# Value products of six cached sequences as two-part fp32r products, split by GpSimd and spread over the pages

## The reference

```
for one sequence:                                 # 8 of them
    ckv = cache_ckv[pages]   (2048, 256) + new (8, 256)
    k   = rmsnorm([ckv @ w_uk | kpe])             # per head, 8 heads
    s   = q . k * SCALE, causal mask
    p   = softmax(s)                              # (8 heads x 8 queries, 2056)
    o_lat = p @ ckv                               # (64, 256): the value product
    o     = o_lat @ w_uv
```

## Time and profile before

| | |
|---|---|
| runs | 1563.53, 1565.51, 1567.21 us; median 1565.51 |
| span of the profiled execution | 1561.6 us, 3.9 us under the median |
| PE busy | 1546.7 us (99%) |
| DVE, ACT, POOL busy | 1042.6, 631.2, 581.8 us |
| granted TensorE clock, mean | 0.998 |
| cached sequences | about 717.5 to 1041.6 us of the span |
| time of the profiled execution itself | not given apart from its span; by the median it would be 1561.6 + 3.9 us |

### The profile page before, as it was taken

How to read it: one execution, slowest core, us unless ns; L and a number is a source line. 1 busy time by engine, 2 the same in 40 slices (tenths; PEclk the granted TensorE clock), 3 DMA queues, 4 the chain that set the end, 5 groups by cost and what they waited for, 6 DMA issues and landing times.

```text
span 1561.6 us, 31760 instructions
## 1 busy us (share of the span) xinstructions
PE 1546.7 (99%) x11182; PEld 1475.9 (95%) x11182; DVE 1042.6 (67%) x1672; ACT 631.2 (40%) x1192; POOL 581.8 (37%) x604
## 2 busy tenths in 40 slices
PE   8999999999999999999999999999999999999998
PEld 8999999999999999588988888888999999999998
DVE  4998888512269975866777777774759988885011
ACT  6444445422221242464654445552434444354110
POOL 3165555445445654320000000013551655554342
PEclk9999999999999999999999999999999999999999
DMA  6133334223223332002122222212222333342222
GB/s 173 51 101 92 94 94 124 69 80 87 80 77 103 83 112 73 1 1 72 52 62 62 61 62 62 58 45 81 82 81 58 105 94 94 94 118 67 75 82 72
DMA packets 231405, 122.29 MB, mean 78 GB/s; under 512 B 28399, under 2 KB 228311, under 8 KB 231300
## 3 DMA queue, kind: packets, MB, share of 16 engines
q1 hardware_dynamic: 230238, 120.30, 27.4%
q10 hardware_dynamic: 1070, 0.74, 0.2%
HBM read 117.79 MB, written 3.58 MB: 78 GB/s over the span
## 4 chain that ended last, share of the span: by engine, by line
PE 93%; DVE 3%; issue 1%; ACT 1%; DMA 1%; SPq 0%; DVEq 0%; ACTq 0%
PE ps L474 40%; PE ps L1439 27%; PE ps L1790 12%; PE ps L1724 4%; PE ps L1710 2%; PE ps L1581 1%; PE ps L1635 1%; PE ps L1610 1%; PE ps L1753 1%; DMA x_nat<-in_x_sample 1%; PE ps L1625 1%; PE ps L1587 1%; PE ps L1592 0%; DVE xs L1999 0%; DVE xs_raw L1984 0%
## 5 line engine op out<-in xcount | busy, mean ns | idle before, releaser
L460 POOL TENSOR_TENSOR w_lobuf<-w_rawbuf,w_hibuf 128x256 fp32r<-128x256 f32 (+2 forms) x336 | 316.8, 974 | 355.1 <-ACT w_hibuf L453 355.1
L1439 PE MATMUL ps<-xs,w 128*128 128x288 f32 x3192 | 427.5, 296 | 2.2 <-DVE w L1913 2.2
L1439 PEld LDWEIGHTS ps<-xs,w 128*128 128x128 f32 x3192 | 426.8, 188 | 2.6 <-issue 2.6
L756 POOL TENSOR_TENSOR w<-w_raw,w 128x256 fp32r<-128x256 f32 x216 | 222.6, 1062 | 222.9 <-DVE w_raw L1901 139.2
L453 ACT ACTIVATE w_hibuf<-w_rawbuf 128x1024 fp32r<-128x1024 f32 (+1 forms) x90 | 104.8, 1164 | 359.6 <-PE ps L474 358.2
L474 PE MATMUL ps<-a_hi,w_hibuf 128*128 128x288 f32 x704 | 152.6, 297 | 0.0
L474 PE MATMUL ps<-a_hi,w_lobuf 128*128 128x288 f32 x704 | 152.1, 297 | 0.0
L474 PE MATMUL ps<-a_lo,w_hibuf 128*128 128x288 f32 x704 | 150.2, 294 | 0.0
L474 PE MATMUL ps<-x_hi,w_hibuf 128*128 128x288 f32 (+1 forms) x672 | 146.1, 299 | 1.6 <-DVE w_lobuf L2073 0.8
L474 PE MATMUL ps<-x_hi,w_lobuf 128*128 128x288 f32 (+1 forms) x672 | 144.5, 296 | 0.0
L474 PE MATMUL ps<-x_lo,w_hibuf 128*128 128x288 f32 (+1 forms) x672 | 144.4, 296 | 0.0
(11 more groups left out here) (320 smaller groups left out, 2722.7 us busy)
## 6 DMA issues: line engine op xcount, KB each, us to landing
w_raw<-in_ffn_w_gu SPq DMA_DIRECT2D x76, 256.0 KB, 2.9
up_rows<-in_ffn_w_gu SPq DMA_DIRECT2D x74, 256.0 KB, 3.1
c_nat<-in_cache_ckv SPq DMA_DIRECT2D x128, 128.0 KB, 2.0
w_rawbuf<-in_w_in SPq DMA_DIRECT2D x58, 256.0 KB, 3.1
w_rawbuf<-in_ffn_w_down SPq DMA_DIRECT2D x32, 384.0 KB, 4.0
w_rawbuf<-in_ffn_w_down SPq DMA_DIRECT2D x32, 320.0 KB, 3.4
w_rawbuf<-in_ffn_w_gu SPq DMA_DIRECT2D x24, 256.0 KB, 3.3
w_rawbuf<-in_w_out SPq DMA_DIRECT2D x16, 256.0 KB, 3.1
```

Source lines behind the costliest of these rows:

```text
L460: ins = pool.tensor_tensor(w_lobuf[:, r, part], w_rawbuf[:, r, part], w_hibuf[:, r % HIS, part].bitcast(F32), ALU.subtract)
L756: ins = pool.tensor_tensor(w7[b][:, slot, 1, part], w7_raw[b][:, slot, 1, part], w7[b][:, slot, 0, part].bitcast(F32), ALU.subtract)
L1439: mm = pe.matmul(ps[:, seven_bank(f, slot), 0:HALF], m, xs[:, slot, n, k, :], start=k == 0 and j == 0, stop=k == KH - 1 and j == 2)
```

## The change

For sequences r = 0 to 5 (those whose softmax runs inside s = 1 to 6, `stacked`), the value product becomes fp32r. The exponentials are written twice: rounded to fp32r in `p_two[..., 0, :]` and in fp32 in `s_buf`; GpSimd subtracts and writes the low part to `p_two[..., 1, :]`. High and low together are one stationary operand of 128 columns. GpSimd also splits each page pair of `c_nat` into `c_hi` (four buffers) and `c_lo` (in place). Each page is then two fp32r matmuls (`c_hi`, `c_lo`) of 256 columns; rows 0 to 63 and 64 to 127 of the result are added at the end. The eight pairs are spread over pages 10 to 14. Sequences 6 and 7 keep the fp32 product. The loads of the first two merge pieces move behind the last page load, and their splits into the last sequence.

```diff
+        STACKED = NS - 2
+        PAIRS, EARLY_PAIRS = NP // 2, len(c_hi)
...
-            for t in range(2):
-                load_merge(t)
...
-                        sp.wait_ge(pages_used, used + (g + 1))
+                        sp.wait_ge(pages_used, used + 2 * (g + 1))
...
+            sp.wait_ge(lat_mm, STACKED)
+            for t in range(2):
+                load_merge(t)
...
+            pool.sem_inc(pages_used, EARLY_PAIRS)
...
+            def split_pair(r, b, j):
+                two = slice(2 * j, 2 * j + 2)
+                made = 2 * j + (1 if j < EARLY_PAIRS else 3)
+                pool.wait_ge(ct_tr, r * PAIRS + (j + 1))
+                pool.wait_ge(pages_used, r * PAIRS + (j + 1))
+                pool.tensor_tensor(c_hi[j % EARLY_PAIRS][:, :, :], c_nat[:, b, two, :], ones[:, 0:1, None].broadcast_to([P, 2, KL]), ALU.mult).then_inc(split_made, 1)
+                pool.wait_ge(split_made, r * SPLITS + made)
+                pool.tensor_tensor(c_lo[:, b, two, :], c_nat[:, b, two, :], c_hi[j % EARLY_PAIRS][:, :, :].bitcast(F32), ALU.subtract)\
+                    .then_inc(split_made, 1)
...
             def squares(s, b, uses, prev, nxt):
+                if prev and stacked(s):
+                    for j in range(EARLY_PAIRS):
+                        split_pair(s - 1, 1 - b, j)
+                    for half in range(2):
+                        probabilities_low(s - 1, 1 - b, half)
+                    for j in range(EARLY_PAIRS, PAIRS):
+                        split_pair(s - 1, 1 - b, j)
+                if not nxt:
+                    split_lo(pool, n_merge, n_merge % RAWS, KD * P)
...
+                for half in range(2):
+                    if stacked(r + 1):
+                        act.activation(p_two[:, t, 0, :], s_buf[:, b, t, :], ACT.Exp, scale=SCALE)
...
+                    ins = act.activation(s_buf[:, b, t, :], s_buf[:, b, t, :], ACT.Exp, scale=SCALE)
...
+                    ins.then_inc(p_done, 1)
...
                     if at(s, pp) == (NS - 1, 1):
+                        split_hi(act, n_merge, n_merge % RAWS, KD * P)
+                    if at(s, pp) == (NS - 1, 2):
                         act.wait_ge(q_split, NS)
                         split_hi(act, n_merge + 1, (n_merge + 1) % RAWS, KD * P, free=False)
...
+                    for j in range(PAIRS):
+                        pe.wait_ge(split_made, pair_made(r, j))
+                        for u in range(2):
+                            t = 2 * j + u
+                            pe.matmul(ps[:, 7, 0:KL], p_two[:, t]..., c_hi[j % EARLY_PAIRS][:, u, :], start=t == 0, stop=False)
+                            mm = pe.matmul(ps[:, 7, 0:KL], p_two[:, t]..., c_lo[:, b, t, :], start=False, stop=False)
+                        mm.then_inc(pages_used, 1)
+                        if j < PAIRS - 1:
+                            yield
...
+                        if prev and stacked(s):
+                            for _ in range({10: 1, 11: 1, 12: 2, 13: 2, 14: 2}.get(t, 0)):
+                                next(soft)
```

More of the change, by code:

```diff
@@ L802, in _ @@
             pool.memset(head_ss[:, :, :, :], 1.0).then_inc(filled, 1)
-            for n in range(n_gate + KD + 2, n_merge + 1):
+            for n in range(n_gate + KD + 2, n_merge):
                 split_lo(pool, n, n % RAWS, KD * P)
@@ L1208, in soft_act @@
                 act.wait_ge(shifted, r + 1)
[L1209 to L1213, removed]
+                for half in range(2):
+                    t = slice(half * NP // 2, (half + 1) * NP // 2)
+                    last = half == 1
+                    if stacked(r + 1):
+                        act.activation(p_two[:, t, 0, :], s_buf[:, b, t, :], ACT.Exp, scale=SCALE)
+                        if last:
+                            act.activation(p_two[0:TS, NP, 0, :], s_buf[0:TS, b, NP, :], ACT.Exp, scale=SCALE)
+                    ins = act.activation(s_buf[:, b, t, :], s_buf[:, b, t, :], ACT.Exp, scale=SCALE)
+                    if last:
+                        ins = act.activation(s_buf[0:TS, b, NP, :], s_buf[0:TS, b, NP, :], ACT.Exp, scale=SCALE)
+                    ins.then_inc(p_done, 1)
+                    yield
             def kpe_copy(s, g):
@@ L1570, in _ @@
             four_gates(KD + 4, q_gate3)
[L1572 to L1573 removed]
+            pe.wait_ge(small_in, 48)
             for i in range(NT):
@@ L1721, in soft_pe @@
                 yield
-                pe.wait_ge(p_done, r + 1)
+                if stacked(r + 1):
+                    for j in range(PAIRS):
+                        pe.wait_ge(split_made, pair_made(r, j))
+                        for u in range(2):
+                            t = 2 * j + u
+                            pe.matmul(ps[:, 7, 0:KL], p_two[:, t].rearrange("p h n -> p (h n)"), c_hi[j % EARLY_PAIRS][:, u, :], start=t == 0, stop=False)
+                            mm = pe.matmul(ps[:, 7, 0:KL], p_two[:, t].rearrange("p h n -> p (h n)"), c_lo[:, b, t, :], start=False, stop=False)
+                        mm.then_inc(pages_used, 1)
+                        if j < PAIRS - 1:
+                            yield
+                    for part in (new_hi, new_lo):
+                        pe.matmul(ps[:, 7, 0:KL], p_two[:, NP].rearrange("p h n -> p (h n)"), part[:, :], start=False, stop=False)
+                    pe.wait_ge(p_summed, r + 1)
+                    pe.matmul(ps[:, 7, KL:KL + 1], den_sum[:, :, :].rearrange("p h n -> p (h n)"), ones[:, 0:1], start=False, stop=True).then_inc(lat_mm, 1)
+                    yield
+                    pe.wait_ge(rows_in, 9 * 16)
+                    pe.wait_ge(lat_scaled, r + 1)
+                    for k in range(2):
+                        tr = pe.transpose(ps[:, 7, k * P:(k + 1) * P], o_lat[:, k * P:(k + 1) * P], ident[:, :])
+                    tr.then_inc(lat_tr, 1)
+                    yield
+                    return
+                pe.wait_ge(p_done, r * 2 + 2)
                 for t in range(NP):
                     mm = pe.matmul(ps[0:HQ, 7, 0:KL], s_buf[:, b, t, :], c_nat[:, b, t, :], start=t == 0, stop=False)
-                    if t % 4 == 3:
+                    if t % 2:
                         mm.then_inc(pages_used, 1)
@@ L1763, in pe_seq @@
                         transpose_pair(s + 1, 1 - b, uses + b, 0)
-                    if prev and pp in (6, 7):
+                    if prev and not stacked(s) and pp in (6, 7):
                         next(soft)
```

83 lines of the change are left out of this document (62 added, 21 removed).

## The result

The changed kernel takes 1583.26 us (median of 4 runs, 1582.09 to 1584.70) against 1565.17 for the kernel before (4 runs, 1563.53 to 1567.21). The ratio is 1.0114, 95% interval 1.0099 to 1.0128. It is slower, by 18 us; 1577.5 was forecast. Its profiled execution took 1582.77, 1.8 us more than its span of 1581.0.

What follows compares the result with a forecast made beforehand. TensorE, busy all 40 us of a sequence's stretch, bounds the kernel. Per sequence -3.5 + 2.6 + 1.5 = +0.6, six +3.6, last sequence +8.6: span 1573.8, plus 3.9 gives 1577.7, stated 1577.5 us; range 1566 to 1592.

Steps and rivals of the forecast that it cites:

- The products: TensorE's 8.03 us value block becomes 34 fp32r matmuls, 4.5 us in all: gain 3.5 us a sequence.
- The rival in which fp32r does not shrink them: Products on TensorE take as long as the fp32 passes (0.22): gain 0.3 instead of 3.5, 1597 us; chance 2%.
- A: TensorE stalls ahead of page 10 for GpSimd's low part of the probabilities: 2.6 us in each of six sequences.
- the rival of a quick GpSimd: GpSimd takes 1.04 us per instruction, no wait for pair 7, 2.4 us at page 10: 1568 us; chance 17%.
- B: TensorE waits at page 14 for GpSimd's splits of pair 7: 1.5 us a sequence taken, 1.2 to 2.1.
- C: TensorE waits after page 13 for the next sequence's page loads: 0.15 us, hidden under B.
- The rest of a sequence: Early GpSimd pairs and extra VectorE and ScalarE work fit into idle time or the waits: nothing added.
- The sum for six sequences: Product gain and the waits at pages 10 and 14 give +0.6 us a sequence, +3.6 for six.
- D: Last sequence, once: late merge load holds ScalarE 9.6 us and TensorE 8.1; with 1.0 for clock, +8.6 us (7 to 11).
- the 3.9 us between span and median: Amount by which the median stood above the profiled span before, added to the predicted span of 1573.8: 1577.7 us.

Runs made afterwards that it cites:

- experiment 11: On top of Experiment 10, one of VectorE's three taps of page pair 6 moved to page pair 4: 1544.89 us, ratio 0.9867 to the kernel before.
- experiment 3: Changed kernel plus a 64x1 exponential on ScalarE after page 5's square, so the exponential's table loads earlier: 1578.46 us, ratio 1.0080.
- Experiment 2: Changed kernel with ten fp32 products of 128x128 put into TensorE's wait at page 10: 1580.85 us, ratio 1.0099.
- Experiment 10: Changed kernel with products from page 11, ScalarE making four high parts, c_nat first, merge splits later, exponential table earlier, c_hi before scores, maximum's subtraction halved: 1559.31 us.
- 7: Changed kernel with ScalarE instead of GpSimd writing c_hi of pairs 4 to 7, at pages 10 to 12: 1579.63 us, ratio 1.0091.
- 6: Changed kernel with SyncE issuing group 0's four c_nat pages ahead of its four kpe_nat pages: 1582.81 us, ratio 1.0111.
- 5: Changed kernel with the pairs' products at pages 11 to 14, two pairs each, instead of from page 10 on: 1583.68 us, ratio 1.0110.
- 4: Changed kernel without the low part of the values, c_hi entering twice, so the output is not the reference's: 1579.47 us, ratio 1.0088.
- Edits 5 and 7 together: Changed kernel with products at pages 11 to 14 and ScalarE writing c_hi of pairs 4 to 7 at pages 11 and 12: 1569.67 us, ratio 1.0028.

## Why the prediction was right, step by step

The sign, the range and the two large terms were right; the forecast fell 5.7 us short of the median.

- **The products.** Gain 3.5 predicted; 3.7 read, and 3.5 in the mean came through in experiment 11. A product of 256 columns with its stationary of 128 has a pitch of 0.12 us (0.125 taken). The rival in which fp32r does not shrink them is out.
- **A, the wait at page 10.** 2.6 predicted, 14.3 / 6 = 2.4 measured. GpSimd's subtraction took 1.27 (1.25 taken), so the rival of a quick GpSimd is out. The reason given for where its length comes from was half right: I put the whole table load into the chain, experiment 3 shows that VectorE's subtraction hid most of it.
- **B, the wait for pair 7.** 1.5 predicted, 2.0 in six sequences measured: 0.3. GpSimd was as predicted: pair 7 was ready 13.4 to 13.5 us after the wait at page 10 ended in sequences 1 to 4 (13.6 predicted, with VectorE beside it), 12.6 and 11.8 in the last two. TensorE wanted it after 11.9 in sequence 4, where the wait was 1.66 (11.5 and 1.2 to 2.1 predicted). In sequences 1 to 3 it came 2.0 to 2.9 us later than predicted, held up by the clock (0.9 to 1.7) and by C, and did not wait for it. The step that failed is "C is hidden under B": C's wait stands ahead of pair 6 on TensorE, so it was B that hid, under C and under the clock, which the sum did not have there.
- **C, the pages.** 0.15 predicted, 5.3 / 6 = 0.9 measured. TensorE came to the transposes 7.8 us after the last product of pair 1 in each sequence (7.95 predicted). The pages took 8.1 to 8.4 after it in sequences 2, 4 and 6 (8.06 predicted), 8.6 and 8.8 in 5 and 3, and 10.0 in 1: SyncE issued the pages 1.7 us apart, but with gaps of 2.0 to 2.8 in those three, and the last page landed in 2.0 to 2.5 (2.0 predicted). The mis-sized term is this chain of transfers; why an issue came late stays open.
- **The clock in the sequences.** The sum had none. It cost about 5 us over six: three pauses of 2.2 to 2.5 us were followed by a stretch with part at 1.2 GHz. With C it is the largest omission. Experiment 2 shows it: with the idle time at page 10 filled, the stretches behind it stayed at 1.00.
- **The rest of a sequence.** "Nothing" was right for this kernel only because the waits gave VectorE time. Experiment 10 shows that VectorE's slowing beside GpSimd (which the sum put at 0.9 us on GpSimd, and only "slower taps" on VectorE) is the next bound.
- The sum for six sequences was +3.6 and is +5.7: the errors -1.3 (A), -7 (B), +5.3 (C, which the sum left out as hidden), +5.1 (clock), -1.2 (products) and +1.3 (two small waits, for `s_buf` and `sq`) offset one another for the most part. That the forecast was nearer than its terms is luck.
- **D, the last sequence.** +8.6 predicted, +10.6 by the offsets; ScalarE waited 9.66 (9.6 predicted), TensorE 8.21 (8.1). The mis-sized part is the clock: 1.0 in the sum, and 2.7 us lost between 1030.5 and 1036, where TensorE worked at 0.50. The Trainium skill, "TensorE: Matmul & The Clock Gate", section "What's actually happening", has idling let the gate throttle TensorE; the prediction said that by this rule the pause would cost about 1.7 more, where the sum has 1.0. The trace agrees with the rule (0.50 behind the pause), and the 2.7 lost are nearer to it than to the sum.
- **From span to median.** The prediction's terms give 1577.7 and it states 1577.5. It took the 3.9 us between span and median as if they were one thing; 1.8 of them are what a time holds beyond its span, the other 2 are that the profiled execution of before was a quick one. The change costs 16.3 us by the traces and 18.1 by the medians; part of the distance between 1577.5 and 1583.3 may be such a difference of executions, and that is left open.

The change holds the gain that it set out for, and it was lost in waits that ended close together. Alone, lifting the one on GpSimd (7), on the pages (6) or at page 10 (2, 3) moved the sequences by 0 to 1.2 us, and moving the products (5) made them 6.1 worse; leaving out 8 of GpSimd's some 20 instructions (4) gave 5.3. Edits 5 and 7 together took 12.1 off the sequences (13.6 in the medians), and with VectorE relieved as well the sequences came to -20.9, for the 6 x 3.5 that the products were to give.

## What to carry to other kernels

When an engine's wait is lifted alone and nothing is gained, look for what else ends within a microsecond or two of it: here limits that ended together paid only when they were moved together. A pause of 2.2 to 2.5 us on TensorE was followed by 1.7 us of lost clock in half of the sequences, so it is priced with that or filled. Work handed to GpSimd was also paid on VectorE while the two ran side by side; put VectorE's movable work where GpSimd rests. And an in-order engine that serves the critical chain should issue a split of a late transfer behind, not ahead of, the chain's own instructions.

## What the runs showed of the hardware

- VectorE beside GpSimd's two-input subtractions: a 128x64 copy 0.93 to 1.33 us for 0.20, a 128x512 tap up to 1.83 for 0.73, while a reduction from 128x512 kept its pace (1.26 for two in either case).
- A GpSimd subtraction of 128x512 to fp32r takes 1.27 to 1.30 us, a product with a broadcast column 1.04, where VectorE has no tap beside them; beside taps they took up to 1.78 and 1.57.
- ScalarE's copy of 128x512 to fp32r from SBUF took 0.58 each (two in 1.15), about half of GpSimd's product (1.04).
- Of the changed kernel's pauses of 2.2 to 2.6 us in sequences 1 to 5 three were followed by a fall of the granted clock (2.20, 2.48, 2.47) and three were not (2.47, 2.48, 2.56); what tells them apart these runs do not show.
